# Key tiles that begin at token 0 in two attentions, and the second attention's projections ahead of a head's scores

## What is computed

```
def causal_block_attention(q, k, v, scale, cum=None):
    ...
    s = jnp.einsum('bhqd,bhkd->bhqk', qb, k) * scale
    if cq is not None:
        s = s + (cq[..., :, None] - cum[:, :, None, :])
    s = jnp.where(key_pos[None, :] <= qpos[:, None], s, -jnp.inf)
    p = jax.nn.softmax(s, axis=-1)
    return jnp.einsum('bhqk,bhkd->bhqd', p, v)
...
o_mla = causal_block_attention(q_m, k_m, v_mla, MLA_SCALE)
log_f = jax.nn.log_sigmoid(f_logit + fox_forget_b)
cum = jnp.cumsum(log_f, axis=-1)
o_fox = causal_block_attention(fox_heads(fq), fox_heads(fk), fox_heads(fv), FOX_SCALE, cum)
...
return h[:, N_META:]
```

## Time and profile before

| what | value |
|---|---|
| median of 3 runs | 1707.81 us (1702.15 to 1707.84) |
| the profiled execution's own time | 1707.32 us |
| its span, first to last instruction | 1705.5 us |
| mean granted TensorE clock | 0.97 of full speed |
| PE busy | 1607.6 us (94%), 10570 matmuls |
| PE weight loads busy | 1415.4 us (83%) |
| DVE busy | 871.8 us (51%) |
| ACT busy | 707.1 us (41%) |

### The profile page before, as it was taken

One profiled execution on the slowest core, in us unless ns is written; L12 is line 12 of the kernel. 1 busy time (PEld: TensorE's weight loads), 2 busy tenths in 40 slices (PEclk: granted clock), 3 DMA queues, 4 the chain that ended last, 5 costly groups with the idle time before them and its releaser, 6 DMA issues.

```text
span 1705.5 us, 24490 instructions
## 1 busy us (share of the span) xinstructions
PE 1607.6 (94%) x10570; PEld 1415.4 (83%) x10570; DVE 871.8 (51%) x1133; ACT 707.1 (41%) x1046; POOL 3.5 (0%) x14
## 2 busy tenths in 40 slices
PE   6999899999989999999997899999998999899988
PEld 5989899999988999988886677688897877668878
DVE  5366776644655554452345687532223665734333
ACT  4464566653333333332235355432223556623232
POOL 0000000000000000000000000000000000000000
PEclk9999999999989999999998999899999999889999
DMA  4411121214322332222232000133222110113321
GB/s 135 148 53 62 52 68 50 63 38 138 111 75 75 99 100 88 86 95 92 93 112 50 1 26 1 50 99 99 90 84 75 41 35 25 50 38 99 99 75 75
DMA packets 130959, 125.48 MB, mean 74 GB/s; under 512 B 20202, under 2 KB 128517, under 8 KB 130469
## 3 DMA queue, kind: packets, MB, share of 16 engines
q1 hardware_dynamic: 130388, 120.36, 22.5%
q0 software_dynamic: 464, 3.56, 0.6%
HBM read 119.66 MB, written 4.26 MB: 73 GB/s over the span
## 4 chain that ended last, share of the span: by engine, by line
PE 88%; DVE 6%; ACT 3%; issue 3%; DMA 0%; SPq 0%; DVEq 0%; ACTq 0%
PE PS L781 72%; PE PS L1087 4%; PE PS L880 3%; PE PS L1044 2%; PE PS L1067 2%; DVE wlo L1655 2%; DVE small L2131 1%; DVE PT L2155 1%; PE PS L800 1%; PE PS L1049 0%; PE PS L1074 0%; PE PS L1050 0%; PE PS L892 0%; ACT Pm L1184 0%; ACT L1189 0%
## 5 line engine op out<-in xcount | busy, mean ns | idle before, releaser
L781 PE MATMUL PS<-zhi,whi 128*128 128x264 f32 (+1 forms) x2000 | 510.8, 317 | 21.8 <-DVE zlo L1716 10.6
L781 PE MATMUL PS<-zlo,whi 128*128 128x264 f32 (+1 forms) x2000 | 505.9, 314 | 0.0
L781 PE MATMUL PS<-zhi,wlo 128*128 128x264 f32 (+1 forms) x2000 | 504.5, 314 | 0.0
L781 PEld LDWEIGHTS PS<-zhi,whi 128*128 128x128 f32 x2000 | 331.4, 191 | 50.2 <-issue 17.9
L781 PEld LDWEIGHTS PS<-zhi,wlo 128*128 128x128 f32 x2000 | 330.3, 191 | 21.5
L781 PEld LDWEIGHTS PS<-zlo,whi 128*128 128x128 f32 x2000 | 329.7, 190 | 21.0
L1655 DVE TENSOR_TENSOR wlo<-raw,whi 128x2048 fp32r<-128x2048 f32 (+2 forms) x113 | 247.5, 2192 | 124.4 <-ACT whi L1184 124.0
L1184 ACT ACTIVATE whi<-raw 128x2048 fp32r<-128x2048 f32 (+2 forms) x113 | 206.9, 1833 | 120.9 <-DMA raw<-in_w_down 40.9
L1184 ACT ACTIVATE Pm<-PS,small 128x144 f32<-128x144 f32 (+3 forms) x128 | 68.8, 540 | 63.7 <-DVE small L2131 61.6
L2131 DVE TENSOR_REDUCE small<-PS 128x1 f32<-128x144 f32 (+3 forms) x128 | 63.5, 502 | 53.4 <-PE PS L1053 52.5
L1067 PE MATMUL PS<-ident,Pm 128*128 128x128 f32 (+1 forms) x448 | 67.3, 279 | 10.4 <-DVE PT L2155 6.2
(11 more groups left out here) (320 smaller groups left out, 2205.3 us busy)
## 6 DMA issues: line engine op xcount, KB each, us to landing
raw<-in_w_in SPq DMA_DIRECT2D x51, 1024.0 KB, 5.2
raw<-in_w_up SPq DMA_DIRECT2D x22, 1024.0 KB, 5.1
raw<-in_w_out SPq DMA_DIRECT2D x8, 1024.0 KB, 5.2
raw<-in_w_down SPq DMA_DIRECT2D x8, 1024.0 KB, 5.2
raw<-in_w_br_mla SPq DMA_DIRECT2D x4, 1024.0 KB, 5.3
raw<-in_w_br_fox SPq DMA_DIRECT2D x4, 1024.0 KB, 5.4
raw<-in_w_down SPq DMA_DIRECT2D x4, 768.0 KB, 4.4
hspill<-hT SPq DMA_DIRECT2D x1, 2112.0 KB, 12.1
```

Of the source, the lines that this page charges most:

```text
L781: ins = mm(o_, l_, r_, start=first, stop=last)
```

## The change

Key blocks now begin at token 0: four of 128 keys and a last one of 16. A score tile is one product over all its keys (two halves for i = 3), and the mask is added to its last 128 columns afterwards. Of the 14 blocks of a head ten are full and four are small: the last 16 keys of each query tile are seen by its last 16 queries alone, so 32 queries by 16 keys are turned, from partitions 96 to 127. Their place in `PT` is cleared once, for the first two heads. The weighing's products shrink in columns. The values are laid out in the same blocks. In the first attention `between` moves behind transposes 0 and score 2 at even h. In the second the projection moves from `between` into `project`, ahead of scores 0 and 1.

```diff
+        KEYS = [P, P, P, P, NM]
+        GROUPS = [[(0, i) for i in range(4)], [(1, i) for i in range(1, 4)], [(2, 2), (2, 3)], [(3, 3)]]
+        PT_STEP = SEQ - P + NM
+        PT_COL = [0] + [SEQ + PT_STEP * j for j in range(4)]
...
                 if i == 3:
-                    cuts, tail = [(PS[:, 5, 0:264], 0), (PS[:, 6, 0:136], 264)], PS[:, 6, 136:264]
+                    cuts, tail = [(PS[:, 5, 0:264], 0), (PS[:, 6, 0:264], 264)], PS[:, 6, 264 - P:264]
                 else:
                     bank = 4 if i % 2 == 0 else 5
-                    cuts, tail = [(PS[:, bank, 0:n - P], 0)], PS[:, bank, n - P:n]
+                    cuts, tail = [(PS[:, bank, 0:n], 0)], PS[:, bank, n - P:n]
...
+                ins = mm(tail, identb[:, :], causalb[:, :], start=False, stop=True, skip_group_check=True)
...
                 for x, (j, i) in enumerate(GROUPS[g]):
-                    o_ = ATT_OFF[i] + (0 if j == 0 else NM + P * (j - 1))
-                    n = NM if j == 0 else P
-                    ins = tr(PS[0:n, 2 + g % 2, P * x:P * (x + 1)], Pm[h % 2][:, o_:o_ + n], ident[:, :])
+                    o_ = ATT_OFF[i] + P * j
+                    ins = tr(PS[:, 2 + g % 2, P * x:P * (x + 1)], Pm[h % 2][:, o_:o_ + P], ident[:, :])
+                if g == 3:
+                    for i in range(QB):
+                        o_ = ATT_OFF[i] + P * (i + 1)
+                        ins = tr(PS[0:NM, 3, P + 32 * i:P + 32 * (i + 1)], Pm[h % 2][96:P, o_:o_ + NM],
+                                 ident[96:P, 96:P])
...
-                for j, (c0, q0, n) in enumerate(((0, 0, 512), (512, 0, 512), (1024, 128, 384), (1408, 256, 256),
-                                                 (1664, 384, 128))):
-                    rows = NM if j == 0 else P
+                for j, rows in enumerate(KEYS):
+                    q0, c0 = max(0, P * j - NM), PT_COL[j]
+                    n = SEQ - q0
...
-                    between(h)
                     for i in range(4):
+                        if i == at(h):
+                            between(h)
                         if 1 <= h <= HEADS:
                             turn(A, h - 1, i)
...
-            attention(mla, mla_project, mla_between)
+            attention(mla, mla_project, mla_between, lambda h: 1 - h % 2)
...
             def fox_project(h):
                 if h == 0:
                     gemm(("xq", 0))
                     gemm(("xk", 0))
                     gemm(("xq", 1))
-
-            def fox_between(h):
-
                 x = h // 2 + 1 + h % 2
                 if x < KT:
                     gemm((("xk", "xq")[h % 2], x))
...
-            attention(fox, fox_project, fox_between)
+            attention(fox, fox_project, lambda h: None, lambda h: 0)
...
-                            n = 512 if g == 1 else 384
-                            V.tensor_copy(PT[x % 2][:, G_COL[g]:G_COL[g] + n], PS[:, 3, 0:n]).then_inc(A.pt_v, 1)
+                            ins = V.tensor_copy(PT[x % 2][:, G_COL[g]:G_COL[g] + G_N[g]], PS[:, 3, 0:G_N[g]])
+                            if g == 3:
+                                tick(ins)
+                                if x < 2:
+                                    tick(V.memset(pt_ends(PT[x]), 0.0))
+                                    settle()
+                                ins = V.tensor_copy(pt_ends(PT[x % 2])[0:NM], PS[0:NM, 3, P:2 * P]
+                                                    .rearrange("p (i c) -> p i c", i=QB)[:, :, NM:2 * NM])
+                            ins.then_inc(A.pt_v, 1)
```

More of the change, by code:

```diff
@@ L611, in build_program, with pt_ends @@
         ATT_N = [144, 272, 400, 528]
-        GROUPS = [[(0, i) for i in range(4)], [(1, i) for i in range(4)], [(2, 1), (2, 2), (2, 3)],
-                  [(3, 2), (3, 3), (4, 3)]]
-        G_COL = [0, 512, 1024, 1408]
+        KEYS = [P, P, P, P, NM]
+        GROUPS = [[(0, i) for i in range(4)], [(1, i) for i in range(1, 4)], [(2, 2), (2, 3)], [(3, 3)]]
+        PT_STEP = SEQ - P + NM
+        PT_COL = [0] + [SEQ + PT_STEP * j for j in range(4)]
+        G_COL = [0] + [c + NM for c in PT_COL[1:4]]
+        G_N = [P * len(g) for g in GROUPS]
+        def pt_ends(t):
+            end = SEQ + 3 * PT_STEP + NM
+            return t[:, end - 4 * PT_STEP:end].rearrange("p (j c) -> p j c", j=4)[:, :, PT_STEP - NM:PT_STEP]
         def s_view(i):
@@ L825, in _, with turn_values @@
             pe.wait_ge(h_copied, KT + 1)
-            def turn_values(src, j, turned, copied, tile_name):
+            def turn_values(src, j, turned, copied, tile_name, tiles):
                 tile_freed(pe, tile_name)
@@ L831, in turn_values @@
                     pe.wait_ge(copied, 2 * j)
[L832 to L835, removed]
+                m0, t0 = tiles
+                tr(PS[0:NM, 5, 0:P], src[:, m0:m0 + NM], ident[:, :])
+                for c in range(4):
+                    ins = tr(PS[:, 4, P * c:P * (c + 1)], src[:, t0 + P * c:t0 + P * (c + 1)], ident[:, :])
                 ins.then_inc(turned, 1)
@@ L1035, in scores @@
                 if i == 3:
-                    cuts, tail = [(PS[:, 5, 0:264], 0), (PS[:, 6, 0:136], 264)], PS[:, 6, 136:264]
+                    cuts, tail = [(PS[:, 5, 0:264], 0), (PS[:, 6, 0:264], 264)], PS[:, 6, 264 - P:264]
                 else:
                     bank = 4 if i % 2 == 0 else 5
-                    cuts, tail = [(PS[:, bank, 0:n - P], 0)], PS[:, bank, n - P:n]
-                for dst, c0 in cuts + [(tail, n - P)]:
-                    last = dst is tail
+                    cuts, tail = [(PS[:, bank, 0:n], 0)], PS[:, bank, n - P:n]
+                for dst, c0 in cuts:
                     c1 = c0 + dst.shape[-1]
                     if A is mla:
-                        ins = mm(dst, qh[h % 2][:, t0:t0 + P], kh[h % 2][:, c0:c1], start=True, stop=not last)
+                        mm(dst, qh[h % 2][:, t0:t0 + P], kh[h % 2][:, c0:c1], start=True, stop=True)
                     else:
@@ L1089, in weigh, with attention @@
                 ins.then_inc(A.o_done, 1)
-            def attention(A, project, between):
+            def attention(A, project, between, at):
                 for h in range(HEADS + 2):
@@ L1501, in attention @@
                                 act.wait_ge(A.o_done, x // 2)
-                            rows, n = (NM, 512) if g == 0 else (P, 384)
-                            A_(PT[x % 2][0:rows, G_COL[g]:G_COL[g] + n], PS[0:rows, 2, 0:n], ACT.Copy)\
+                            A_(PT[x % 2][:, G_COL[g]:G_COL[g] + G_N[g]], PS[:, 2, 0:G_N[g]], ACT.Copy)\
                                 .then_inc(A.pt_a, 1)
@@ L2117, in _ @@
                     n = ("mv", i, j)
-                    rows = NM if i == 0 else P
+                    rows = KEYS[i]
                     tile_done(dve, n)
```

26 lines of the change are left out of this document (12 added, 14 removed).

## The result

| | before | changed |
|---|---|---|
| median of the runs, us | 1704.98 (4 runs beside it) | 1744.95 |
| lowest and highest, us | 1701.34, 1707.84 | 1741.46, 1745.78 |
| the profiled execution, us | 1707.3 | 1741.46 |
| its span, us | 1705.5 | 1739.6 |
| its granted clock, mean | 0.970 | 0.955 |

The ratio is 1.0232, with a 95% interval of 1.0202 to 1.0261: the kernel is 2.3% slower. Forecast were 1738 us, between 1715 and 1755.

A forecast was written before the change was run, and what follows sets the result against it. TensorE was taken to bound the kernel, carrying 88% of the span. The terms, 29 + 1.5 + 4 + 12 - 3.5 - 12 = +31 us on the profiled 1707.3 us, gave 1738 us, range 1715 to 1755.

The forecast's parts named there:

- first attention: Smaller weighing, score tile 0, small transposes and the key projection's move sum to 12.6 us saved; 12 taken.
- chain, even and odd heads (29 + 1.5): Second attention: accumulator waits through split, maximum 2 and exponential 2; 3.6 us more at eight heads, 0.3 at five odd ones.
- wait for `wlo`, three heads: Projections of heads 2, 6 and 10 wait longer for a weight's low part: 1.3 us a head, 4 us.
- clock: Second attention: TensorE's idle gaps lower the clock at the next projection's start; 12 us lost, between 0 and 17.
- heads 13 to 17: End of the second attention, order unchanged: three smaller weighings, two at half the clock, save 3.5 us.
- the bound of 17: Upper bound of the clock loss in the second attention: ten heads at 1.7 us each, 17 us.
- The key projection's new place: First attention, even heads: behind score 2 its 0.53 us wait goes; 0.2 us kept for 7 heads, 1.4 us gained.
- The small transposes: Four of 32 by 16 a head: gain of 0.15 us taken, 2.4 us in the first attention.
- Nothing for the products up to head 12: Second attention: fewer score and weighing products count as no gain, as other engines set a head's time there.
- the chain without the clock: Rival: the second attention's chain holds but the clock doesn't fall in the gaps; +19 us, 1726 us; chance 0.21.
- Faster: Rival: projection covers the exponential's wait and the split doesn't delay the accumulator in the second attention; 1670 us; chance 0.09.

The follow-up runs named there:

- experiment 9: Changed kernel with unused identity transposes as filler in nearly every gap of the second attention, also ahead of the wait for `wlo`: 1721.71 us, ratio 1.0086.
- Experiment 5: Changed kernel with twelve unused identity transposes ahead of transposes 2 and 3 at heads 4, 6, 8, 10, 12 and 14 of the second attention: 1726.06 us, ratio 1.013.
- experiment 4: Changed kernel with the first attention's key projection back ahead of transposes 0 at even heads too: 1741.32 us, ratio 1.0209 to the kernel before.
- experiment 2: Kernel before with only the second attention's projection moved ahead of scores 0 and 1, old blocks kept: 1767.74 us, ratio 1.0372.
- experiment 3: Changed kernel with the rounding (split) of the next head's queries and keys moved to the start of a head: 1698.7 us, ratio 0.996 to the kernel before.

## Why the prediction was right, and where its terms were off

The sign, the place and the mechanism came as written, and 1744.95 us lies 7 over the forecast of 1738; the sizes by part are these. Measured values are differences between the two profiled executions, whose spans differ by 34.1 us.

| term | forecast | measured |
|---|---|---|
| first attention | -12 | -7.9 |
| chain, even and odd heads (29 + 1.5) | +30.5 | +30.7 (head 0 5.0, seven at 3.4 to 3.6, five at 0.17) |
| wait for `wlo`, three heads | +4 | +3.6 |
| clock | +12 | +15.6 (19.0 in projections, -3.4 in two weighings) |
| heads 13 to 17 | -3.5 | -3.4 |
| outside both attentions | 0 | -4.7 |

The last row is the stretches up to the first attention (-4.2), the middle without its projection (+1.0) and the end (-1.5). They hold no part of the change, and nothing in it would move them. The rows add up to 33.9 us, 0.2 under the 34.1. The first attention gave 4.1 us less than forecast and the clock took 3.6 more; 4.7 us the other way came from stretches that the change doesn't touch. So that the total comes as near as 3 us is in part luck. The median of the runs lies another 3.5 us over the profiled execution.

**The chain** was the main term, and it fell on its number: 8.0 us from first score to projection, put together from head 14's 3.73 us and head 8's 3.8 us, is 8.0 in the row above. For odd heads 8.6 was forecast and it is 8.46 (1417.51 to 1425.97). The wait for `wlo` was put at 2.6 us behind the other chain; heads 5 and 9 show 10.99 us from first score to projection (1448.25 to 1459.24), 2.53 over an odd head, and head 1 10.95, where 8.0 would be due; heads 2, 6 and 10 before had 1.5 (11.85 us against head 4's 10.34).

**The clock was the mis-sized term.** I had 17 us as the upper bound and took 12, for some stretches had been low before. The twelve projections among heads 0 to 12 take 19.2 us longer in sum than at full clock, against 0.2 before, and experiment 9, whose heads run the same chain, gets 17 of them back. To take something off for stretches that were low before was right: heads 9 and 11 before had their weighings at a low clock, 5.00 us each for 3.31, and in the changed kernel these weighings take 2.60 within a chain of unchanged length. That is 3.4 us, where I took 5. Timeline, kernel before, head 11's weighing:

```profile
1443.46 5.07 PE L1087 MATMUL PS<-PT,vtok 16*64 16x512 f32 x20
1448.46 0.50 PE L781 MATMUL PS<-zhi,whi 128*128 128x512 f32 x1
```

What failed is the bound of 17, ten gaps at 1.7. I left out the odd heads 3, 7 and 11, since their chain adds only 0.3 us; their projections lose 1.5 us each. Experiment 5 shows that this belongs to the even head's gaps: with only these filled, the odd head's projection is at full clock too. So the gaps of an even head cost its pair 2.7 us (1.2 and 1.5), not 1.7, and about 2.4 are lost where `wlo` is waited for. Head 12, which I counted, has no projection behind it. The rule of the Trainium skill that I had cited here ("TensorE: Matmul & The Clock Gate", Part 1: throttled is the default, activity releases it) agrees with experiments 5 and 9, where activity without any use kept the clock at 1.00 and 0.96. It isn't all that moves the clock, for in the earlier trace rows the granted clock is 0.57 in a window where PE is busy 4.00 of 4 us.

**The first attention** was over-sized by 4 us. An odd head gained 0.92 (10.52 to 9.60), as the sum of 0.7 for the weighing (3.31 to 2.60) and 0.2 for score tile 0. The last weighing, which runs at a low clock in both traces (granted 0.50 and 0.59), gained 2.0 (6.37 to 4.36). Even heads gained nothing: between 6.75 and 7.5 us, and between 6.63 and 7.35 before. The key projection's new place, which I had put at a gain of 1.4 us, costs 2.5 (experiment 4). Timeline of an even one, changed kernel:

```profile
981.13 0.94 PE L1050 MATMUL PS<-kh,qh 128*128 128x400 f32 x2 [0.69 <-ACT Pm L1190]
...
981.93 0.49 PE L788 MATMUL PS<-ckhi,whi 128*128 128x264 f32 x2
```

Score 2 waits 0.69 us for exponential 0, where the key projection had waited 0.53 for VectorE's copy. I had foreseen this wait "in part" and kept 0.2; it ate that, and the 0.2 of the smaller tile, and the small transposes' gain. Experiment 4 puts the old wait back, and most even heads are 0.14 us shorter for it. So I read that the exponentials and copies set an even head's time, and that what TensorE saves there isn't on the path; no run took their work away to show it.

**The small transposes** were bounded between a gain of 0.44 and a loss of 0.36 us a head, and 0.15 taken. Timeline, changed kernel:

```profile
965.95 0.49 PE L1070 MATMUL PS<-ident,Pm 128*128 128x128 f32 x3
966.28 1.06 PE L1050 MATMUL PS<-kh,qh 128*128 128x264 f32 x4
...
967.23 0.50 PE L1070 MATMUL PS<-ident,Pm 128*128 128x128 f32 x3
967.66 0.28 PE L1074 MATMUL PS<-ident,Pm 32*16 32x32 f32 x4
967.87 0.50 PE L788 MATMUL PS<-cqhi,whi 128*128 128x512 f32 x1
```

Four of them take 0.21 us from start to start, against 0.44 for four of the old ones. But three whole transposes take 0.33 us when a score follows them (965.95 to 966.28), and 0.43 when the small ones do (967.23 to 967.66), so the small ones cost 0.31 with the 0.10 ahead of them, and the gain is 0.13 a head. By the rule of the Trainium skill ("TensorEngine Tiling (Array Packing)", Tiling Modes: changing the mode drains TensorE) they were to lose 4 us. The 0.10 us ahead of the first small one agrees with a drain of that size; behind the last one none shows. Two slips stand in that estimate: 0.36 us at 16 heads is 5.8 us, not 4, and both loads of the earlier trace rows lie inside the weighing, where the array's shape doesn't change. Neither is in the sum.

**Nothing for the products up to head 12** held for the change as it stands, since the chain was built from rows and came out at 8.0. But the reason given, that the other engines set the time whatever TensorE does, was too broad. In experiment 2 the same chain takes 8.36 and 9.50 us with the old products: I read that in an odd head the weighing is partly on the path.

Of the rivals, "the chain without the clock" was put at 1726 us; experiment 9, with the clock kept by force, gives 1721.71. "Faster" was decided at 4.4 us from first score to projection; experiment 3 brought it to 4.72 by moving the split, and lies 0.4% under the kernel before.

## What to carry to other kernels

Before moving independent work on the bound engine, ask which chain of other engines it covers; build the exposed stretch from rows of a place that already lacks the cover (here head 14), and add the clock it loses behind the gap, for the following stages too. If the order can't be helped, issue the covered chain earlier, or fill the gap. And take a change of two parts apart before judging it: one part here was worth some 20 us and the other cost 60.

## What the runs showed of the hardware that was not expected

- Idle time costs twice. Behind two waits of 1.8 to 1.9 us within 8 us the following projection was 1.19 us longer (6.86 for 5.67), and the odd head's behind it 1.5 us; with only the even head's gaps filled, both were at their full-clock time (5.68 and 5.91).
- Products that compute nothing made the kernel faster: 336 transposes of the identity in the gaps gave 17 us in heads 0 to 12, with the granted clock of the second attention going from 0.83 to 0.96. Filling the gaps of every second head was enough for a pair of heads.
- The clock was also low with TensorE at work: the same weighing took 3.31 us in heads 3, 5 and 7 before and 5.00 in heads 9 and 11, with PE busy 4.00 of 4 us at a granted clock of 0.57.
- Transposes of 32 by 32 elements on 32 rows and 16 columns of the array cost 0.05 us each from start to start, about half of the others' 0.11, and 0.10 us once ahead of the first, 0.31 us for four.
